# Weights in DRAM as tiles with 8 KB runs, and a second pair of column blocks as seven block products in the first feed-forward layer

## What is computed

```python
D_MODEL, SEQ, D_FF = 1024, 256, 2816

def swiglu(x, w_gate, w_up, w_down):
    return (jax.nn.silu(x @ w_gate) * (x @ w_up)) @ w_down

f = swiglu(rms_norm(h, ffn1_pre_g[i]), ffn1_w_gate[i], ffn1_w_up[i], ffn1_w_down[i])
h = h + 0.5 * rms_norm(f, ffn1_post_g[i])
m = hybrid_mixer(rms_norm(h, mix_pre_g[i]), w_in[i], rpb[i], ...)
```

## Time and profile before

| | |
|---|---|
| time, median of 3 executions | 1591.63 us (1591.54 to 1591.74) |
| span of the profiled execution, first to last instruction | 1590.1 us |
| TensorE (PE) busy | 1579.6 us, 7659 instructions |
| VectorE (DVE) busy | 1120.3 us |
| ScalarE (ACT) busy | 864.4 us |
| GpSimd (POOL) busy | 144.4 us |
| read from DRAM | 339.12 MB, 214 GB/s over the span |
| packets under 2 KB | 179168 of 256949 |

### The profile page before, as it was taken

How to read it: one execution, slowest core, us unless ns; L and a number is a source line. 1 busy time by engine, 2 the same in 40 slices (tenths; PEclk the granted TensorE clock), 3 DMA queues, 4 the chain that set the end, 5 groups by cost and what they waited for, 6 DMA issues and landing times.

```text
span 1590.1 us, 18859 instructions
## 1 busy us (share of the span) xinstructions
PE 1579.6 (99%) x7659; PEld 1317.3 (83%) x7659; DVE 1120.3 (70%) x1081; ACT 864.4 (54%) x907; POOL 144.4 (9%) x148
## 2 busy tenths in 40 slices
PE   9999999999999999999999999999999999999998
PEld 6888897788888888888988888888888998888886
DVE  6785566677875678965668896678856657688864
ACT  7554447556653766642655665365543435455651
POOL 0241000001100010001010100001000131001000
PEclk9999999999999999999999999999999999999999
DMA  9995574479955798663649985699655554599860
GB/s 320 266 236 186 184 244 134 159 231 253 279 184 173 257 280 252 193 241 97 238 159 287 237 243 213 212 241 270 228 185 193 193 174 151 190 276 233 258 211 27
DMA packets 256949, 341.40 MB, mean 215 GB/s; under 512 B 9952, under 2 KB 179168, under 8 KB 256736
## 3 DMA queue, kind: packets, MB, share of 16 engines
q1 hardware_dynamic: 228848, 301.82, 58.1%
q0 software_dynamic: 27648, 38.12, 12.4%
q10 hardware_dynamic: 368, 0.27, 0.1%
HBM read 339.12 MB, written 1.05 MB: 214 GB/s over the span
## 4 chain that ended last, share of the span: by engine, by line
PE 98%; DMA 1%; DVE 0%; ACT 0%; SPq 0%; issue 0%; DVEq 0%
PE bank L845 25%; PE bank L858 24%; PE bank L849 21%; PE bank L907 4%; PE bank L912 4%; PE bank L909 4%; PE bank L795 3%; PE bank L862 3%; PE bank L941 2%; PE bank L944 2%; PE bank L943 2%; DMA whole<-in_gla_w_in 0%; DMA whole<-in_ffn_w_up 0%; PE bank L1330 0%; PE bank L1120 0%; PE bank L1139 0%
## 5 line engine op out<-in xcount | busy, mean ns | idle before, releaser
L1891 DVE TENSOR_TENSOR split<-whole,split 128x2048 fp32r<-128x2048 f32 (+2 forms) x329 | 705.2, 2162 | 215.3 <-ACT split L1448 213.3
L1448 ACT ACTIVATE split<-whole 128x2048 fp32r<-128x2048 f32 (+1 forms) x313 | 582.7, 1877 | 293.4 <-DMA whole<-in_ffn_w_out 60.9
L845 PE MATMUL bank<-split,xh 128*128 128x512 f32 x1052 | 288.0, 395 | 0.0
L858 PE MATMUL bank<-split,xh 128*128 128x512 f32 x1052 | 282.1, 390 | 0.0
L849 PE MATMUL bank<-split,xl 128*128 128x512 f32 x880 | 235.8, 390 | 0.0
L858 PEld LDWEIGHTS bank<-split,xh 128*128 128x128 f32 x1052 | 197.2, 188 | 41.8 <-DVE split L1891 0.3
L845 PEld LDWEIGHTS bank<-split,xh 128*128 128x128 f32 x1052 | 193.0, 188 | 40.5 <-issue 2.8
L849 PEld LDWEIGHTS bank<-split,xl 128*128 128x128 f32 x880 | 165.2, 188 | 35.4
L845 PE MATMUL bank<-split,th 128*128 128x512 f32 x524 | 143.7, 392 | 0.0
L849 PE MATMUL bank<-split,tl 128*128 128x512 f32 x524 | 142.2, 389 | 0.0
L858 PE MATMUL bank<-split,th 128*128 128x512 f32 x524 | 142.1, 389 | 0.0
(11 more groups left out here) (312 smaller groups left out, 1776.4 us busy)
## 6 DMA issues: line engine op xcount, KB each, us to landing
whole<-in_ffn_w_in SPq DMA_DIRECT2D x192, 512.0 KB, 7.6
whole<-in_ffn_w_out SPq DMA_DIRECT2D x40, 1024.0 KB, 5.2
whole<-in_ret_w_in SPq DMA_DIRECT2D x24, 1024.0 KB, 5.1
whole<-in_ffn_w_gate SPq DMA_DIRECT2D x45, 512.0 KB, 7.9
whole<-in_ffn_w_up SPq DMA_DIRECT2D x45, 512.0 KB, 8.9
whole<-in_ffn_w_down SPq DMA_DIRECT2D x20, 1024.0 KB, 5.2
whole<-in_w_in SPq DMA_DIRECT2D x16, 1024.0 KB, 5.5
whole<-in_ffn_w_in POOLq DMA_DIRECT2D x32, 512.0 KB, 8.6
```

The costliest lines, as they stand in the source:

```text
L845: pe.matmul(o[:, :], tokens(0, k), whi[:, k, :], start=start and k == 0, stop=False, skip_group_check=True)
L858: ins = pe.matmul(o[:, :], tokens(0, k), wlo[:, k, :], start=False, stop=end, skip_group_check=True)
L1448: act.activation(split[s][:, 0:n], whole[r][:, 0:n], ACT.Copy).then_inc(hi.mark(i), 1)
L1891: dve.tensor_tensor(split[r][:, c0:c1], whole[r][:, c0:c1], split[s][:, c0:c1].bitcast(F32), ALU.subtract).then_inc(lo.mark(*what), 1)
```

## The change

Two things. **The weights** are laid out on the host, as plain reordering: every tile of the plan is contiguous per partition, so that a partition's 2048 elements are one run of 8 KB (4 KB for half tiles), and gate and up columns of a block lie side by side. So each load is one DMA where gate and up tiles had two, the accumulating ones too; the first tile's parts are two of 256 KB and one of 512 KB, all on SP, and ScalarE's queue issues none of them. **The order of `f1`** changes to `LATE_PAIRS` with the pairs 3, 4 and 7, 8, and POOL's accumulating DMAs for both groups are placed in its list.

```diff
-LATE_PAIR = (
+LATE_PAIRS = (
     ("tile", 0, 0), ("tile", 0, 1), ("tile", 1, 0), ("tile", 1, 1), ("turn", 0),
     ("tile", 2, 0), ("tile", 2, 1), ("turn", 1), ("token sums",),
-    ("tile", 3, 0), ("tile", 3, 1), ("turn", 2), ("blocks",),
-    ("tile", 4, 0), ("tile", 4, 1), ("turn", 3),
-    ("product", 0, "b11"), ("tile", 5, 0),
-    ("product", 0, "t1"), ("tile", 5, 1), ("turn", 4),
-    ("product", 0, "t2"), ("tile", 6, 0),
-    ("product", 0, "b22"), ("tile", 6, 1), ("turn", 5),
-    ("product", 0, "t3"), ("tile", 9, 0), ("turn", 6),
-    ("product", 0, "b21"), ("tile", 9, 1), ("turn", 8),
-    ("product", 0, "t4"), ("tile", 10, 0), ("tile", 10, 1), ("turn", 9), ("turn", 7))
+    ("tile", 5, 0), ("tile", 5, 1), ("turn", 2), ("blocks",),
+    ("product", 0, "b11"), ("tile", 6, 0),
+    ("product", 0, "t1"), ("product", 0, "t2"), ("tile", 6, 1), ("turn", 5),
+    ("product", 0, "b22"), ("product", 0, "t3"), ("tile", 9, 0),
+    ("product", 0, "b21"), ("product", 0, "t4"), ("turn", 4), ("tile", 9, 1), ("turn", 6),
+    ("product", 1, "b11"), ("turn", 3), ("tile", 10, 0),
+    ("product", 1, "t1"), ("product", 1, "t2"), ("tile", 10, 1),
+    ("product", 1, "b22"), ("product", 1, "t3"), ("turn", 9),
+    ("product", 1, "b21"), ("product", 1, "t4"), ("turn", 8), ("turn", 7))
...
-LATE, TWO = Order(LATE_PAIR, 7), Order(TWO_PAIRS, 3, 7)
+LATE, TWO = Order(LATE_PAIRS, 3, 7), Order(TWO_PAIRS, 3, 7)
...
         def sp_tile(sp, i):
             freed(sp, load_after[i])
             w, b = tiles[i], load_to[i]
-            dst = lanes(whole[b][:, 0:w.k * w.width], w.k)
-            for src, c0 in w.pieces:
-                sp.dma_start(dst[:, :, c0:c0 + src.shape[2]], src).then_inc(raw_in[b].mark(i), 16)
+            sp.dma_start(whole[b][:, 0:w.k * w.width], w.src).then_inc(raw_in[b].mark(i), 16)
...
-            sp.dma_start(dst[:, 0:1, 0:256], gate[:, 0:1, :]).then_inc(tile_0[0].mark("all"), 16)
-            sp.dma_start(dst[:, 1:2, 0:256], gate[:, 1:2, :]).then_inc(tile_0[1].mark("gate"), 16)
-            sp.dma_start(dst[:, 1:2, 256:512], up[:, 1:2, :]).then_inc(tile_0[1].mark("all"), 16)
-            for src, c0 in tiles[0].pieces:
-                sp.dma_start(dst[:, 2:4, c0:c0 + 256], src[:, 2:4, :]).then_inc(raw_in[load_to[0]].mark(0), 16)
+            for k in range(2):
+                c = slice(512 * k, 512 * k + 512)
+                sp.dma_start(dst[:, c], tiles[0].src[:, c]).then_inc(tile_0[k].mark("all"), 16)
+            sp.dma_start(dst[:, 1024:2048], tiles[0].src[:, 1024:2048]).then_inc(raw_in[load_to[0]].mark(0), 16)
...
             for n in range(8):
-                if n == 2:
+                if n == 0:
                     pool_sum(pool, "t1", group["f1", 0].t1)
-                if n == 7:
+                if n == 4:
                     pool_sum(pool, "t3", group["f1", 0].t3)
                 pool.wait_ge(lo.sem, lo.of(6 + n))
                 pool_bias(0, n)
             for n in range(8):
+                if n == 3:
+                    pool_sum(pool, "t1", group["f1", 1].t1)
+                if n == 7:
+                    pool_sum(pool, "t3", group["f1", 1].t3)
                 pool.wait_ge(lo.sem, lo.of(14 + n))
                 pool_bias(1, n)
...
+def by_columns(w, width=512):
+
+    K, N = w.shape
+    return w.reshape(K // 512, 4, P, N // width, width).transpose(3, 0, 2, 1, 4)
```

More of the change, by code:

```diff
@@ L415, in build @@
-        plan_ffn_2("b1", 1, 1)
+            plan_rows(name + "d", A[f"w_{name}_down"], A[f"w_{name}_down_head"])
+        w_mix, w_gla, w_ret = A["w_mix"], A["w_gla"], A["w_ret"]
+        plan_ffn("f1")
+        plan_x("mvx", w_mix, (2, 3))
+        plan_x("mqk", w_mix, (0, 1))
+        plan_x("mg", w_mix, (4, 5, 6, 7))
+        for c in range(2):
+            plan_x("brp", A["w_branch_pool"], (c,))
+            plan_x("bra", A["w_branch_attn"], (c,))
+        plan_rows("mo", A["w_mix_out"])
+        plan_ffn("f2")
@@ new lines, in build @@
+        plan_rows("pp", None, A["w_ple_project"])
+        plan_x("pg", A["w_ple_gate"], (0, 1))
+        plan_ffn("a0")
+        plan_x("gv", w_gla, (2, 3))
+        plan("gl", A["w_gla_low"], 8, 16)
+        plan_x("gq", w_gla, (0,))
+        plan_x("gk", w_gla, (1,))
+        plan_x("gr", w_gla, (4, 5))
+        plan_rows("go", A["w_gla_out"])
+        plan_ffn("a1")
+        plan_ffn("b0")
+        plan_x("rv", w_ret, (4, 5, 6, 7))
+        plan_x("rqk", w_ret, (0, 1, 2, 3))
+        plan_x("rg", w_ret, (8, 9, 10, 11))
@@ L459, in give_blocks @@
             for i in range(first, end):
-                if tiles[i].pieces:
+                if tiles[i].src is not None:
                     events.append((load_key[i] - LOAD_LEAD, "load", i))
@@ L619, in x_part, with second_tile @@
                     x_in[t][g].mark(g), 16)
-            def second_tile(k, sig, what):
-                second = lanes(whole[load_to[1]][:, :], 4)
-                for src, c0 in tiles[1].pieces:
-                    sp.dma_start(second[:, k:k + 2, c0:c0 + 256], src[:, k:k + 2, :]).then_inc(sig.mark(what), 16)
+            def second_tile(c, sig, what):
+                sp.dma_start(whole[load_to[1]][:, c:c + 1024], tiles[1].src[:, c:c + 1024]).then_inc(sig.mark(what), 16)
             assert load_after[0] == load_after[1] == NONE
@@ L629, in sp_program @@
             x_part(0, 1)
-            second_tile(2, raw_in[load_to[1]], 1)
+            second_tile(1024, raw_in[load_to[1]], 1)
             x_part(1, 1)
             for i in sorted(range(2, NT), key=load_key.get):
-                if tiles[i].pieces:
+                if tiles[i].src is not None:
                     sp_tile(sp, i)
@@ L660, in pool_sum @@
                 pool.wait_ge(sum_in[m].sem, sum_in[m].n)
[L661 to L662 removed]
+            pool.dma_start(whole[b][:, :], addend[i], accum_op=ALU.add).then_inc(sum_in[m].mark(i), 16)
         def pool_program(pool):
```

102 lines of the change are left out of this document (44 added, 58 removed).

## The result

The changed kernel takes **1600.34 us** (median of 5 runs, 1600.05 to 1601.71) against 1591.74 for the kernel before, measured beside it (5 runs, 1591.54 to 1592.51): ratio 1.0054, 95% interval [1.0043, 1.0065], 8.6 us slower. The forecast was 1597.3 in 1591.0 to 1602.5. The profiled execution is the slowest of the five: 1601.71 us, its span 1599.9, 9.8 us more than the span of before; the spans of the other four lie between 1598.2 and 1598.9.

The account below looks back on a forecast made before the run. TensorE, busy 1579.6 of 1590.1 us, was taken as the bound, with VectorE to watch. Terms -2.7 - 0.8 - 0.4 + 3.2 + 2.7 + 3.7 = +5.7 on 1591.6 gave 1597.3 us, range 1591.0 to 1602.5.

Parts of the forecast that it names:

- its own sign of being wrong: Forecast wrong if idle times sum under 3 us, granted clock leaves 2.4 GHz, or later layers change over 1 us.
- Matmuls: First layer's second pair as seven products: 12 matmuls fewer on TensorE, -2.7 us.
- First group: Tile (6,0) and t2: TensorE waits for low parts queued on VectorE behind split sl, 2.6 + 0.6 us, +3.2.
- VectorE over the second group: From t2's sum to turn 7, VectorE's queued work ends after TensorE is ready: +2.7 us.
- the masks: Second group: nine POOL mask additions hold VectorE up by 0.41 us each, +3.7 us; bounds 0 and 5.1.
- The masks by a page: Alternative estimate by the exclusive-lock rule: nine masks cost VectorE up to their full length, 6.7 us, time 1600.3.
- Start: Kernel start: fewer issues ahead on SP let the second x piece land earlier, -0.8 us; bounds nothing and 1.3.
- Gated attention: TensorE's 0.67 us idle at 770.9 shrinks as the landing heading its chain gets faster, -0.4 us.
- rival (c): Waits of 3 to 6 us bring back the 1.2 GHz clock, 1.7 us each; 1600.7 with two; chance 0.08.
- The price of a stop: On TensorE every wait that comes costs its full length, since no later slack takes it up.
- The late accumulating transfer: Second group, t3's accumulating DMA: covered by VectorE's lateness, cost nothing; 1 us if landing takes 3 us more.

Follow-up runs that it names:

- blocks_early: Changed kernel with the step blocks put between tiles (5,0) and (5,1): 1595.85 us, ratio 1.0026 to the kernel before.
- one_pair_x_first: layout_alone with the second x piece issued ahead of the 512 KB rest of the first tile: 1592.24 us, ratio 1.0004 to the kernel before.
- layout_alone: The new tiled weights with the first layer's old order (one pair): 1591.59 us, ratio 0.9997 to the kernel before.
- masks_late: Changed kernel with POOL's sixteen mask additions made to wait for down tiles of the same layer: 1601.65 us, ratio 1.0054 to the kernel before.
- order_alone: The old weights in 1 KB runs with the new two-pair order of the first layer: 1604.09 us, ratio 1.0076 to the kernel before.
- masks_down: Changed kernel with no mask addition released before the fifth down tile: 1596.29 us, ratio 1.0036 to the kernel before.
- respaced_b_fill: Changed kernel with blocks earlier, masks at down tiles, short first transfers, second group respaced, seven scratch matmuls before the first layer's last turn: 1590.54 us, ratio 0.9997.
- fill_wait: Changed kernel with sixteen scratch matmuls ahead of the first layer's last turn, in TensorE's longest stop: 1599.65 us, ratio 1.0048 to the kernel before.

## Why the prediction was right and where it was wrong

It was right in sign and range, and 3.0 us short of the median. Its mechanism, VectorE's queue with the masks on top, was right too; by its own sign of being wrong, that the granted clock leaves 2.4 GHz, it was not the whole of it. By its own steps:

- **Matmuls, -2.7**: as forecast.
- **First group, +3.2**: brackets of 2.46 and 0.35, with restarts 3.4. The mechanism (sl ahead of the low part of (6,0)) is shown by blocks_early.
- **VectorE over the second group, +2.7, and the masks, +3.7**: stops of 1.45 and 3.86, with restarts 5.9 for 6.4. VectorE's own work was 29.3 us for 29.1. The masks cost 2.6 for 3.7, and the excess has a plain cause: the row of 121.34 in the earlier trace rows that I took for two subtractions of 128x1024, due 2.35, merges one of 128x2048 and one of 128x1024, due 3.42; they were held up by 0.27 us, not 1.34. With that the mean is (0.58 + 0.54 + 0.27) / 6 = 0.23, nine make 2.1.
- **The masks by a page.** The Trainium skill, SBUF — State Buffer, section "Who interferes with whom", has whichever of the two issues second fully blocked; by that rule I had 6.7 us for the masks, as an estimate. Here the measured 2.6 decides: one of the two does wait, as the rule says, but mostly POOL (9.67 us for five masks of 0.74). The time by that estimate, 1600.3, meets the median by luck: the 4.1 us too much for the masks stand in for what was left out elsewhere.
- **Start, -0.8: this step failed.** Fewer issues stand ahead of the second x piece on SP (four for six, not three), it was issued 1 us sooner, and it landed later. I priced the queue of issues. The bytes ahead of it counted, as one_pair_x_first shows, the same 1 MB of the first tile as before, and with them the length of the pieces or the queue that issues them. It is +0.8 us for the start of the transposes on the mean of the profiles, +2.7 at turn 2 in the profiled execution of this kernel.
- **Gated attention, -0.4**: -1.0 came, but not from the layout, as layout_alone shows. The sign of this term was luck.
- **The clock** was kept apart as rival (c), for waits of 3 to 6 us and with 0.08. It was no alternative to my case but its consequence: a stop of 3.9 us, part of the 6.4 that my own sum had for the second group, lowered the clock each time it was profiled, for 1.6 us, what (c) priced at 1.7. Leaving it out was the second error. The Trainium skill, TensorE: Matmul & The Clock Gate, "Why this matters for your kernels", warns of long idle gaps for this; the trace agrees, and here stops of 1.6 to 2.5 us already did it at times.
- **The price of a stop**: I counted idle time one to one; it costs 0.29 us more, 1.2 for four. That this cancels the 1.1 us too much for the masks is luck.
- **The late accumulating transfer, 0 (to +1)**: right for this kernel, where VectorE's lateness covered it. masks_late shows it as the next thing in line, and order_alone as a stop of its own.

With these five corrections (+1.6 start, +1.6 clock, +1.2 restarts, -1.1 masks, -0.6 gated attention) 1597.3 becomes 1600.0; the median is 1600.34. This is an account made afterwards. The start's term is the transposes' 0.8 us, of which 0.3 to 0.7 are left at turn 2, and clock, restarts and gated attention are those of one execution, so that it closes does not prove each term.

## What to carry to other kernels

A second pair in seven products saves TensorE 2.7 us and gives VectorE 12.8 us more to do, in a stretch in which it has no slack; it needs the work of the other engines moved with it (blocks and masks, worth 8.9 us together), and even then what is left, 1.3 us, is within the interval of the measurement. A stop that a forecast contains must be carried on: add the restart, and the chance of the low clock, at 1.5 to 2.5 us. Here it fell behind 1 of 10 stops of 1.4 to 2.0 us, 5 of 8 of 2.2 to 2.5, and all four of 3.9. And a row of a merged view says the shape of its first instruction only; before a duration is divided, ask for the shapes apart.

## What was not expected of the hardware

- The clock fell behind one stop of 1.62 us and stayed behind one of 2.95; behind six stops of 2.43 to 2.46 us at the same place it fell three times. The length of the stop alone does not decide. The spread of 7 us in masks_down follows its mean granted clock. Elsewhere the spread does not tell: 1.7 us in the changed kernel, with such stops, 4.4 in order_alone, where four of five executions have the same mean clock, and 3.5 in respaced_b_fill, whose profile has no stop over 0.7 us behind the start.
- The stop in the gated attention is 0.28 to 1.62 us in the four kernels with one pair (before among them), 0.74 in fill_wait, and absent in the other nine with two pairs, old layout or new. Its cause stays open.
- A transfer of 1 MB lands as fast in 2 KB runs as in 8 KB runs in the gated attention (6.29 and 6.30 us). What the runs change is how busy the DMA engines are with the same bytes. The columns of a window are the stretch, its length, busy time of TensorE, its weight loads, VectorE, ScalarE and POOL, then granted clock, DMA share and GB/s. First the kernel before, then layout_alone, with the same order:

```profile
70.00:112.00 42.00, 42.00 (x192) 34.78 (x191) 36.46 (x26) 26.96 (x24) 19.98 (x21) 1.00 0.92 235
70.00:112.00 42.00, 42.00 (x193) 34.74 (x192) 36.30 (x26) 27.38 (x24) 19.33 (x21) 1.00 0.80 235
```

Both move 235 GB/s, with gate and up tiles in 1 KB runs at a share of 0.92 and in 8 KB runs at 0.80. With the new order, order_alone (1 KB runs) and then the changed kernel:

```profile
70.00:112.00 42.00, 42.00 (x195) 34.74 (x194) 35.13 (x28) 24.01 (x24) 19.26 (x21) 1.00 1.11 287
70.00:112.00 42.00, 41.65 (x191) 34.13 (x190) 35.47 (x28) 25.39 (x26) 15.78 (x20) 1.00 1.00 302
```

The long runs move 302 GB/s at a share of 1.00, the short ones 287 at 1.11.
